# Cumulated forget logarithms as two rows of the fox queries and keys, fillers at four waits of TensorE, and the banks of the first down product in order of age

## The reference

```python
def first_block(...):
    h = concatenate([zeros, meta, x])
    h = h + 0.5 * swiglu(rms_norm(h, g_ffn1), w1_gate, w1_up, w1_down)      # 1024 -> 2816 -> 1024
    h = h + hybrid_mixer(rms_norm(h, g_mix), ...)
    h = h + 0.5 * swiglu(rms_norm(h, g_ffn2), w2_gate, w2_up, w2_down)

def hybrid_mixer(u, ...):
    c_q, c_kv, k_pe, fox_qkv, f_logit = split(u @ w_in)
    ...                                             # 8 MLA heads, 96 wide, keys with their own norm
    o_mla = block_causal_attention(q, k, v, 1 / sqrt(96), key_valid)
    log_f = log_sigmoid(f_logit + b_forget)
    cum = cumsum(log_f, axis=1)                     # one number for each token and fox head
    o_fox = block_causal_attention(fq, fk, fv, 1 / sqrt(64), key_valid, cum)   # 8 fox heads, 64 wide
    return concatenate([o_mla, o_fox]) @ w_out

# in block_causal_attention, for each block of 128 queries:
    s = (q @ k.T) * scale
    if cum is not None: s = s + (cum[query] - cum[key])
    p = softmax(where(mask, s, -1e30)); o = p @ v

# the second block: ada = silu(c) @ ada_w, recurrence and convolution, then the PEER layer:
    eidx, gate = top 16 of 128 x 128 experts for each of 8 heads
    y = sum over the experts: gate * gelu(u_tab[eidx] . h) * v_tab[eidx]
```

## Time and profile before

| | us |
|---|---|
| median of 3 runs | 1654.2 (1653.34 to 1654.63) |
| profiled execution, its own time | 1657.73 |
| its span | 1655.9 |
| mean granted clock of TensorE | 0.965 |
| PE busy | 1506.1 (91%) |
| DVE busy | 1020.7 (62%) |
| POOL busy | 563.7 (34%) |
| ACT busy | 543.4 (33%) |

### The profile page before, as it was taken

One profiled execution on the slowest core, in us unless ns is written; L12 is line 12 of the kernel. 1 busy time (PEld: TensorE's weight loads), 2 busy tenths in 40 slices (PEclk: granted clock), 3 DMA queues, 4 the chain that ended last, 5 costly groups with the idle time before them and its releaser, 6 DMA issues.

```text
span 1655.9 us, 22700 instructions
## 1 busy us (share of the span) xinstructions
PE 1506.1 (91%) x8260; PEld 1153.0 (70%) x8260; DVE 1020.7 (62%) x2102; ACT 543.4 (33%) x1101; POOL 563.7 (34%) x361
## 2 busy tenths in 40 slices
PE   6999989999999999999999988998977868787877
PEld 6999988778899998998889986444533323333333
DVE  4455354756334425897993847767667676758556
ACT  4343343444344434544115442212121212121213
POOL 4555345000144442001001413554544545354441
PEclk9999999989999999999999999999999989899899
DMA  6666789997789998899876857999999999999996
GB/s 250 249 240 230 258 315 393 314 321 271 266 321 373 367 365 315 327 374 378 315 283 218 321 224 299 415 427 427 426 427 426 427 427 427 427 427 427 427 427 266
DMA packets 98868, 571.87 MB, mean 345 GB/s; under 512 B 10976, under 2 KB 11104, under 8 KB 49120
## 3 DMA queue, kind: packets, MB, share of 16 engines
q1 hardware_dynamic: 60768, 298.15, 49.2%
q0 software_dynamic: 36864, 268.45, 38.5%
q10 hardware_dynamic: 1152, 4.17, 0.7%
HBM read 569.68 MB, written 135.27 MB: 426 GB/s over the span
## 4 chain that ended last, share of the span: by engine, by line
PE 69%; DMA 18%; DVE 7%; issue 2%; ACT 2%; POOL 1%; another core or an unknown queue 1%; ACTq 0%; POOLq 0%; DVEq 0%
DMA arena<-pairs,eidx 17%; PE ps L2323 12%; PE ps L1782 9%; PE ps L1784 9%; PE ps L1783 9%; PE ps L2128 5%; PE ps L1833 2%; PE ps L1835 2%; PE ps L1834 2%; PE ps L2296 2%; PE ps L2079 2%; PE ps L2145 2%; DVE arena L1661 1%; PE ps L1797 1%; DMA ring<-pairs,eidx 1%
## 5 line engine op out<-in xcount | busy, mean ns | idle before, releaser
L2323 PE MATMUL ps<-arena 128*128 128x512 f32 x884 | 424.6, 635 | 87.0 <-ACT arena L1081 87.0
L2323 PEld LDWEIGHTS ps<-arena 128*128 128x128 f32 x884 | 175.5, 203 | 322.5 <-issue 204.7
L1661 DVE CUSTOM_DVE_ANT_0 arena<-arena 128x1024 f32<-128x1024 f32 x221 | 268.8, 1223 | 163.4 <-DMA arena<-pairs,eidx 163.2
L718 POOL DMA_INDIRECT arena<-pairs,eidx x221 | 262.0, 1186 | 310.4 <-PE ps L2323 250.1
L686 POOL TENSOR_TENSOR w_lo<-ring,w_hi 128x1024 fp32r<-128x1024 f32 x82 | 218.8, 2670 | 423.7 <-DVE w_lo L1165 343.8
L1782 PE MATMUL ps<-u_hi,w_hi 128*128 128x256 f32 (+1 forms) x1056 | 305.1, 289 | 12.3 <-DVE u_lo L1134 11.7
L1784 PE MATMUL ps<-u_hi,w_lo 128*128 128x256 f32 (+1 forms) x1056 | 303.2, 287 | 0.0
L1783 PE MATMUL ps<-u_lo,w_hi 128*128 128x256 f32 (+1 forms) x1056 | 302.8, 287 | 0.0
L735 ACT ACTIVATE w_hi<-ring 128x1024 fp32r<-128x1024 f32 x188 | 198.0, 1056 | 170.4 <-PE ps L1835 77.5
L1782 PEld LDWEIGHTS ps<-u_hi,w_hi 128*128 128x128 f32 x1056 | 201.4, 191 | 15.6 <-issue 12.6
L1784 PEld LDWEIGHTS ps<-u_hi,w_lo 128*128 128x128 f32 x1056 | 202.2, 191 | 0.0
(11 more groups left out here) (332 smaller groups left out, 2330.9 us busy)
## 6 DMA issues: line engine op xcount, KB each, us to landing
ring<-in_stream SPq DMA_DIRECT2D x126, 1024.0 KB, 7.0
pairs<-in_peer_u SPq DMA_DIRECT2D x128, 512.0 KB, 7.5
pairs<-in_peer_v SPq DMA_DIRECT2D x128, 512.0 KB, 8.9
arena<-in_ada SPq DMA_DIRECT2D x32, 768.0 KB, 6.4
arena<-in_stream SPq DMA_DIRECT2D x4, 1024.0 KB, 9.0
arena<-pairs,eidx POOLq DMA_INDIRECT x221, 15.8
h<-in_x_t SPq DMA_DIRECT2D x1, 1088.0 KB, 7.5
arena<-in_keys ACTq DMA_DIRECT2D x1, 1024.0 KB, 7.6
```

Of the source, the lines that this page charges most:

```text
L718: pool.indirect_dma_start(slot_of(n), None, pairs, bass.IndirectOffsetOnAxis(ap=eidx[:, n:n + 1], axis=0)).then_inc(landing(n)[0], 16)
L1661: dve.tensor_tensor_reduce(row, row, hf[:, n % HEAD_ROWS // TOPK, :], 1.0, 0.0, ALU.mult, ALU.add, dots[:, n % HEAD_ROWS:n % HEAD_ROWS + 1 ...
L2323: mm = pe.matmul(ps[:, Y_BANKS[j // TOPK] + half, :], diag[:, n % DIAGS, :], slot_of(n)[:, D + half * 512:D + half * 512 + 512], start=(hd ...
```

## The change

1. **Fox scores.** cum / FOX_SCALE and 1 become two more rows of each head's query tile, 1 and −cum / FOX_SCALE two more rows of its key tile, so that the one product over 66 rows (even heads: rows 0 to 65) or 128 rows (odd heads: 0 and 1 for these, 64 to 127 for the head, zeros between) gives the scores with the difference. The products with `sel` go. `fk` has a tile for each head, which DVE writes in eight halves of 64 rows and not in four tiles. POOL clears and sets the tiles (six memsets, `fox_set`), in front of the last three splits of its part of the stage; two memsets of DVE go. As soon as DVE has the cumulated rows (`cum_done` 4, with one operation more than before), POOL copies them by 16 DMAs of one row each, and PE waits for all of them (`cum_in`) ahead of unit 16.
2. **Fillers.** `keep_warm(n)` issues n products of 256 columns whose result nobody reads: 9 after norm(0), 12 after norm(1), 5 after the sums before the second block's first product, and three of 224 columns before the fourth key norm.
3. **Banks by age.** The first down product of each FFN takes its output tiles in the order in which the banks were freed and waits for `glu_done` once for two banks, not once for all.
4. **adaLN.** 20 pair copies stand ahead of the last eight loads and four behind them; DVE folds in behind `scale_p(n)` for n = 7, 10, ..., 28.
5. **Layout.** Ring, h and u lie behind the small constants, with padding up to a multiple of 256 bytes. The ring starts at byte 30208 of each partition and before at 16512; the arena starts at 80384 in both.

```diff
-BEFORE_ADA = 24
+BEFORE_ADA = 20
+AFTER_ADA = 4
+ADA_UNITS = list(range(7, 31, 3))
...
+        to_boundary = -(-(-nc.sbuf_base // 32) * 32) % BOUNDARY
+        if to_boundary:
+            sb("pad", [P, to_boundary // 4])
+        ring = sb("ring", [P, RING, PIECE])
...
+        CUM_ROWS = [slice(HD, HD + 2), slice(0, 2)]
+        FOX_ROWS = [slice(0, HD + 2), slice(0, 2 * HD)]
...
+            for n in range(AFTER_ADA):
+                pair_up(at + n)
+            at += AFTER_ADA
...
+            pool.wait_ge(half_used, half_number(0, BASE["w_out"], 0))
+            pool.memset(fqz[:, :, :], 0.0).then_inc(fox_set, 1)
+            pool.memset(fk[0:HD, 1::2, :], 0.0).then_inc(fox_set, 1)
+            pool.wait_ge(fox_set, 2)
+            for e in range(2):
+                pool.memset(fqz[CUM_ROWS[e], e::2, :], 1.0).then_inc(fox_set, 1)
+                pool.memset(fk[CUM_ROWS[e], e::2, :], 1.0).then_inc(fox_set, 1)
+            pool.wait_ge(fox_set, 6)
+            pool.wait_ge(cum_done, 4)
+            for hd in range(HEADS):
+                row = CUM_ROWS[hd % 2].start
+                of = slice(FL_ROW + hd, FL_ROW + hd + 1)
+                pool.dma_start(fqz[row:row + 1, hd, :], cumz[of, xc]).then_inc(cum_in, 16)
+                pool.dma_start(fk[row + 1:row + 2, hd, :], ncumz[of, :]).then_inc(cum_in, 16)
...
-            then(dve.memset(cumz, 0.0), lb_step)
...
-            then(dve.memset(fqz[:, :, :], 0.0), lb_step)
...
+            dve.wait_ge(fox_set, 6)
...
-                dve.scalar_tensor_tensor(fk[:, j, :], praw[:, 8 + j, :], V("g_fk"), ps[:, FK_BANKS[j], 0:T],
-                                         ALU.mult, ALU.mult).then_inc(fox_done, 1)
+                for e in range(2):
+                    r = slice(HD * e, HD * e + HD)
+                    dve.scalar_tensor_tensor(fk[r, 2 * j + e, :], praw[r, 8 + j, :], V("g_fk")[r], ps[r, FK_BANKS[j], 0:T],
+                                             ALU.mult, ALU.mult).then_inc(fox_done, 1)
...
-            dve.tensor_scalar(ncumz, cumz, -1.0, None, ALU.mult).then_inc(cum_done, 1)
+            dve.tensor_scalar(cumz[fr, :], logf[fr, 1, :], 1.0 / FOX_SCALE, None, ALU.mult).then_inc(cum_done, 1)
+            dve.tensor_scalar(ncumz[fr, :], logf[fr, 1, :], -1.0 / FOX_SCALE, None, ALU.mult).then_inc(cum_done, 1)
...
-                if n % 2 and n >= units // 2:
-                    ada_add(KT // 2 + n // 8, n // 2 % ADA_Q)
+                if n in ADA_UNITS:
+                    i = ADA_UNITS.index(n)
+                    ada_add(KT - 2 + i // ADA_Q, i % ADA_Q)
...
-                pe.wait_ge(glu_done, FT * (k + 1))
+
+                def sums_by_age():
+
+                    for age in range(RING):
+                        pe.wait_ge(glu_done, FT * (k + 1) - (RING - 1) + age)
+                        slot = (base + FT - RING + age) % RING
+                        yield from (2 * slot, 2 * slot + 1)
...
-                        for m in range(KT):
+                        for m in sums_by_age() if first else range(KT):
...
+            def keep_warm(n):
+
+                for i in range(n):
+                    pe.matmul(ps[:, 7, 0:SEQ], C("mean_d"), con[:, 0:SEQ], start=True, stop=True)
...
             norm(0)
+            keep_warm(9)
             ffn(0)
             norm(1, KT - LAG)
+            keep_warm(12)
...
             for hd in range(HEADS):
+                if hd == 3:
+                    for i in range(3):
+                        pe.matmul(ps[:, NORM_BANKS[3], T:T + KEPT], C("mean_d"), con[:, 0:KEPT], start=True, stop=True)
                 key_norm(hd)
...
-                        pe.wait_ge(cum_done, 3)
-                    pe.matmul(dst, fqz[:, f, q], fk[:, f // 2, 0:keys_n], start=True, stop=False)
-
-                    pe.matmul(dst, cumz[:, X0 + t * P:X0 + (t + 1) * P], C("sel")[:, f:f + 1].broadcast_to([P, keys_n]), start=False, stop=False)
-                    pe.matmul(dst, C("sel")[:, f:f + 1].broadcast_to([P, P]), ncumz[:, 0:keys_n], start=False, stop=False)
+                        pe.wait_ge(cum_in, 2 * HEADS * 16)
+                    own = FOX_ROWS[f % 2]
+                    pe.matmul(dst, fqz[own, f, q], fk[own, f, 0:keys_n], start=True, stop=False)
...
             norm(3, KT - LAG)
             ada_sums(24, 48)
+            keep_warm(5)
```

More of the change, by code:

```diff
@@ L55 @@
 WIDE = 64
+BOUNDARY = 256
+KEPT = 224
 ARENA_SLOTS = 11
@@ L104 @@
 CONSTS = [("ident", P), ("mean_d", P), ("mean_256", P), ("mean_128", P), ("mean_64", P), ("mean_96", P),
-          ("ones", P), ("rot", P), ("cos", T), ("sin", T), ("neg_mask", P), ("iota", TOPK), ("sel", HEADS)]
+          ("ones", P), ("rot", P), ("cos", T), ("sin", T), ("neg_mask", P), ("iota", TOPK)]
 CON = {}
@@ L143, in constants @@
     put("neg_mask", np.where(np.arange(P)[None, :] > np.arange(P)[:, None], NEG, 0.0).astype(np.float32))
-    sel = np.zeros((P, HEADS), np.float32)
-    for h in range(HEADS):
-        sel[FL_ROW + h, h] = 1.0 / FOX_SCALE
-    put("sel", sel)
     put("iota", np.broadcast_to(np.arange(TOPK, dtype=np.float32), (P, TOPK)))
@@ L194, in program @@
         ps = ctx.enter_context(nc.psum_tensor("ps", [P, 8, 512], F32))
-        ring = sb("ring", [P, RING, PIECE])
-        h = sb("h", [P, KT, T])
-        u_all = sb("u", [P, KT * T])
-        u = u_all[:, :].rearrange("p (k t) -> p k t", t=T)
         cols = sb("cols", [P, N_COLS])
@@ L209, in program @@
         warm = sb("warm", [P, 1])[:, :]
+        to_boundary = -(-(-nc.sbuf_base // 32) * 32) % BOUNDARY
+        if to_boundary:
+            sb("pad", [P, to_boundary // 4])
+        ring = sb("ring", [P, RING, PIECE])
+        h = sb("h", [P, KT, T])
+        u_all = sb("u", [P, KT * T])
+        u = u_all[:, :].rearrange("p (k t) -> p k t", t=T)
         ARENA = 34816
         arena_at = -(-nc.sbuf_base // 32) * 32
+        assert arena_at % BOUNDARY == 0 and 4 * PIECE % BOUNDARY == 0
         arena = sb("arena", [P, ARENA])
@@ L281, in program @@
         fqz = view(HEADS, SEQ)
-        fk = view(HEADS // 2, T)
+        fk = view(HEADS, T)
         vM = view(3, HEADS * HD)
@@ L441, in program @@
         cum_done = sem("cum_done")
+        fox_set = sem("fox_set")
+        cum_in = sem("cum_in")
         kpe_done = sem("kpe_done")
@@ L1304, in _ @@
             then(dve.tensor_tensor(logf[fr, 3, :], logf[fr, 0, :], logf[fr, 2, :], ALU.subtract), cum_done)
-            then(dve.tensor_tensor_scan(cumz[fr, :], C("ones")[fr, 0:1].broadcast_to([HEADS, T]), logf[fr, 3, :], 0.0,
+            then(dve.tensor_tensor_scan(logf[fr, 1, :], C("ones")[fr, 0:1].broadcast_to([HEADS, T]), logf[fr, 3, :], 0.0,
                                         ALU.mult, ALU.add), cum_done)
-            dve.tensor_scalar(ncumz, cumz, -1.0, None, ALU.mult).then_inc(cum_done, 1)
+            dve.tensor_scalar(cumz[fr, :], logf[fr, 1, :], 1.0 / FOX_SCALE, None, ALU.mult).then_inc(cum_done, 1)
+            dve.tensor_scalar(ncumz[fr, :], logf[fr, 1, :], -1.0 / FOX_SCALE, None, ALU.mult).then_inc(cum_done, 1)
             def soft_max(n):
@@ L1943, in fox_key @@
                 if j:
-                    pe.wait_ge(fox_done, (4, 8, 9)[j - 1])
+                    pe.wait_ge(fox_done, (4, 8, 10)[j - 1])
                 spread(ps[:, FK_BANKS[j], :], frms, 1, j, token_tiles(0, 3)).then_inc(fk_mm, 1)
@@ L1999, in key_norm @@
                 mm.then_inc(kn_mm, 1)
-            pe.wait_ge(fox_done, 12)
+            pe.wait_ge(fox_done, 16)
             for t, (at, n) in enumerate(token_tiles(0, 3)):
```

## The result

The changed kernel takes 1677.05 us (median of 4 executions, 1672.98 to 1680.94), the kernel before 1654.32 (1653.34 to 1654.63): the ratio is 1.0138, 95% interval 1.0113 to 1.0163, so 22.7 us slower. The prediction was 1650, faster.

The account below looks back on a forecast made before the run. A serial front of 1000 us, set by PE almost everywhere, then a gather phase of fixed bytes. Banks −2.8, norm fillers −0.7, ring −0.8 and mixer +0.2 sum to −4.1, about 1650 us, range 1640 to 1657.

Parts of the forecast that it names:

- +2.0 for units at half clock behind it: Softmax units behind the first addition's wait for its load run at half clock: +2.0 us.
- the first addition: Behind unit 7 in the mixer, DVE waits for an adaLN load until 356.6, PE idles some 6 us: +3.5.
- The fox rows: Fox units without the sel products: a pair falls from 5.00 to about 3.8 us, −9.5, bounds −8.6 and −11.3.
- Banks by age: First down product of both feed-forward layers: PE's waits behind DVE's glu_lo vanish, −2.8 us, bounds −3.2 and −1.5.
- Norm fillers and key fillers: PE's waits at the norms: −0.6 at norm(0), −0.1 at norm(1), 0 at norm(3); key norms at full clock: 3.4 us gained.
- Additions: DVE's adaLN additions behind every third softmax unit: 0.6 us each, seven without the first, +4.2, bounds 0 and +12.7.
- POOL's rows: POOL's 16 row copies, wanted by unit 16: landing taken as 6 us, all in by 362, cost 0 us.
- rival (c): Row copies land after 369, each microsecond beyond is on the path; 376 would give +7, 1657; chance 0.05.
- Rival (a): The first addition's adaLN load comes in time: mixer −8.1, sum −12.4, 1641.8 us; chance 0.33.
- Rival (b): DVE bounds the softmax units, additions not absorbed: seven at 1.81 cost 12.7, sum +4.4, 1658.6 us; chance 0.12.
- The ring: Gathers into ring slots that start at a multiple of 256 bytes: 0.03 us each for 35, −0.8, bounds 0 and −1.2.
- its own sign: The prediction is wrong as a whole if the gather phase changes in length by more than 2 us.

Follow-up runs that it names:

- gap fillers: Changed kernel plus three fillers of 256 columns ahead of the first turn of probabilities, in PE's pause of 1.59 us: 1679.70 us, ratio 1.0151.
- the runs with and without the stall: Changed kernel with gap fillers, 20 against 16 pair copies ahead of the last eight adaLN loads: 1679.70 and 1640.25 us.
- long fillers: Changed kernel with gap fillers, plus two fillers of 144 or 272 columns in each fox unit: 1668.23 us, ratio 1.0078.
- 16 pair copies: Changed kernel with 16 pair copies ahead of the last eight adaLN loads and 8 behind: 1640.25 us with gap fillers, 1641.16 without.
- the small filler: Changed kernel with gap fillers and old adaLN part, plus one filler of 128 columns behind each fox unit's mask: 1645.71 us, ratio 0.9937.

## Why the prediction was wrong

**The step that failed** is the term "+2.0 for units at half clock behind it" in the part on the first addition. The place, the cause and roughly the size of the stall stood there: a wait of DVE until 356.6 was forecast, and in the kernel with gap fillers it lasted until 353.4, 4.6 us with PE idle as long, for some 6 forecast. What failed was the assumption that the clock would be back after about as many products as at the key norms. At half clock a pair of units takes 6.6 us, PE counts as busy throughout, and the clock doesn't come back for 85 us in the gap-filler kernel and 106 in the profiled execution of the changed kernel. The term should have been about 32: the twelve pairs that follow at 6.6 us against 3.9. With the 4.6 of the wait that is 37, and the runs with and without the stall are 36 us apart.

I had a row for what half clock costs, but took the return of the clock near 342 in the kernel before as a rule for every place. The runs show that it isn't one: behind the key norms it came back after 10.2 us in three profiles (before, fox rows alone, placement alone), and in the changed kernel without key fillers, with the same instructions 2 us earlier, it didn't come for 112.6 us.

**The fox rows** were priced by the time of the two products that go, and these had a second use: with them, or with fillers of their size, the clock returned soon after the first fox unit in three kernels (before + adaLN part, long fillers, all but fox rows); without them it never did before the output products, in six profiles, and came some 3 to 6 us after these had begun. Where the adaLN part was as before, the faster units also came too early to loads behind the first: DVE waited 1.69 us, PE 1.58, and the clock fell (changed + gap fillers, old adaLN part). Such waits were not among my terms: I let the additions' loads after the first come in time. The gain itself was right where the clock holds: 4.0 us a pair with additions in it, 3.8 + 0.4 forecast.

**The ways of stalling.** In the changed kernel's profile the fall came from another pause than in my sum, 0.53 + 1.59 us at the start of the units, where DVE still had the four operations on the logarithms ahead of its first maximum. The same pause was there with 16 pair copies, and the clock held. With gap fillers and 20 pair copies the clock passed that place and fell at the addition. The profiled execution of the changed kernel has a mean clock of 0.941, its three others 0.949 and 0.950, as the kernel with gap fillers has 0.948 to 0.954: so these three would fit a fall at the addition, but have no trace. Either way the units run at 0.50, and the times are nearly the same.

**Point by point.** Banks by age: the waits of 2.8 us are 0.0, as forecast. Norm fillers and key fillers: the products behind the mixer's input (L1912) begin 1.75 us earlier, at 286.93 for 288.68, against −2.1 from one bank wait and the norms; the clock at 332 to 333 is 1.00; the key norms' 2.6 us is there. All these with the placement gave 8.8 us, where I had 7.7. Additions: 0.6 us each was about right or too much, 8 of them with three in MLA units gave 1.1 us in sum. POOL's rows: landing 5.6 us after their issue of 0.5 us each, all by 350, so no part of the loss, and rival (c) didn't happen. Rival (a) is the kernel with 16 pair copies: forecast 1641.8 for a load in time, 1640.25 and 1641.16 measured. Rival (b), DVE as the bound, was the forecast of a loss, but with a wrong mechanism. The ring: +0.4 us, −1.8 to +2.5 by the interval, where I had −0.8 (0.03 for each of 35 gathers is 1.0, so that sum was a little off). The gather phase was to keep its length within 2 us, and 656.2 became 651.8: by its own sign the prediction was wrong there too. The sign was too narrow, since the four kernels with the old placement have 654.3 to 657.5 (leaving out the fox rows alone) and the eleven with the new one 651.8 to 654.5, one profile each. That would fit some 2 us for the placement, which the ten executions of the placement alone don't bear out.
The Trainium skill's rule on transactions (DMA: Bandwidth & Descriptors, section "How a descriptor splits into AXI transactions"), by which I had estimated −2.6, isn't seen in the placement alone, whose interval ends at −1.8 us. It would fit the kernel with the fox rows alone, where the arena starts 224 bytes past a multiple of 256: 420 GB/s for 427 is 1.6% less, about half of the 3% of my estimate.
The Trainium skill (TensorE: Matmul & The Clock Gate, section "HAM oscillation — how this bites in real kernels") tells of waits for a DMA between thin groups of products after which each group starts at half clock. This case's fall behind a wait for a load agrees; but here one such wait of 4.6 us was followed by 85 us at half clock, with PE counted as busy.

What stays open: why the clock came back near 342 in the kernel before and not in the changed one without key fillers; why it fell in the fox units of the rows alone with hardly a pause of PE; why it falls behind a pause of some 1.5 us in one profile and holds in another; what the small filler does; and which of the two pauses acts in which execution of the changed kernel, since only one of its executions has a trace.

## What to carry to other kernels

Before taking products out of a stretch, look whether the clock is regained there, and ask of every stall not how long it is but what the units behind it can do at half clock: if these don't bring the clock back, a wait of 1.6 us can cost the rest of the stage. Price a stall twice, once with the clock back soon and once with the whole stage at half clock, and let the second be an end of the range. Where a unit becomes faster, go through all loads that it consumes, not just the first. And where an experiment takes a part out of a kernel, look whether tiles behind it have moved, and read the stages apart before the whole time is put down to one of them.

## What the hardware showed that I had not expected

- The clock stayed at 0.50 from 339.0 to 444.8 with PE busy 70 of 70 us between 360 and 430. A PE that is busy by the trace's count did not bring it back.
- The same softmax units held full clock for 60 us with 57.86 us busy, and didn't regain it once it was lost, with 70.00 of 70 (16 and 20 pair copies, both with gap fillers).
- Two products of 144 or 272 columns more per unit, useless ones, brought it back within 9.5 us (fox units from 374.2, clock back at 383.7).
- A DMA issue on POOL for one row of 1 KB within SBUF takes 0.48 us, not the 1.19 of a gather, and it landed after 5.6 us while the DMA engines had 0.96 to 1.06 of their share.
- With the arena 32 bytes lower, off a multiple of 256 bytes, the gathers ran at 420 GB/s for 427, 11 us of 656; one profile, and not tested by itself.
